# A hybrid decoder trunk on one core: attention norm applied inside TensorE's transposes, and VectorE's program written out for both layers

## The chip, the cores and the metric

The kernel runs on one core of a Trainium2 chip. The metric is the device time of one execution in microseconds (us). Lower is better.

## The reference, cut to what matters

Two layers, one after the other, over 256 tokens with 1024 features, all in fp32. Each layer normalises x, makes one wide projection that feeds three kinds of attention, merges them into x, adds a mixture of experts, and adds a gated embedding:

```python
def rmsnorm(x, g):
    xf = x.astype(jnp.float32)
    y = xf * lax.rsqrt(jnp.mean(xf * xf, axis=-1, keepdims=True) + NORM_EPS)
    return (y * g.astype(jnp.float32)).astype(x.dtype)

def hybrid_layer(x, ...):
    h = rmsnorm(x, attn_norm)
    (a_q, ..., gate_logits) = jnp.split(h @ w_in, IN_OFFSETS, axis=-1)
    ...
    x = x + merged @ w_o
    x = x + hierarchical_moe(rmsnorm(x, ffn_norm), ...)
    x = x + jax.nn.sigmoid(rmsnorm(x, ple_norm) @ w_ple_gate) * (p_i @ w_ple)
```

The mixture has 32 experts in 4 groups. Each token takes the best group and the best two experts in it, so 512 token-expert pairs are spread over 32 experts by comparing router logits.

## The kernel before

The 256 tokens are two tiles of 128 (t = 0, 1), with tokens on the partitions in `x` and `h`. Matmuls need features on the partitions, so each normalised x is transposed into `hT` (8 blocks of 128 features, 256 tokens). The program is written for five engines by hand, and each engine has its own instruction stream; they meet only through semaphores. What the text calls the layer loop is a hardware loop (`Fori`) over the two layers in each of the five streams. A value that a semaphore must reach depends on the layer; inside the hardware loop it is worked out with register instructions.

There are three norms in a layer, and `n` numbers them: 0 attention, 1 experts (ffn), 2 embedding gate (ple). For each tile ScalarE squares x with a running sum and takes the root (`rms_of_x`; all of ScalarE's operations are recorded at line 1210), and sends `rms_ready`. What follows differs:

- Norm 0: VectorE takes the reciprocal (L1500) and writes the normalised tile to `h` (`normed`, L1502, 128x1024), in the block order of the transposes. TensorE transposes the 8 blocks of `h` (`transpose_tile`, L668, with `h_block`).
- Norms 1 and 2: TensorE transposes x itself (`x_block`, every eighth feature), and the reciprocal root is applied later, to the router's logits or to the gate. For norm 1 VectorE still writes `h` with `normed`, since the gather of rows for the experts reads it (L1104).

A tile is transposed in two halves of four blocks, each into one bank of `ps`; VectorE takes each half out with the norm's gain (`take_hT`, L1510). With the four takes of norm 0 done, TensorE starts the wide projection (`channel_group`, L695, then L674 for token-major products).

The layer then goes through the three attention branches, the merge and the output projection (L674). Between the two products of the output projection's second tile TensorE transposes x's tile 0 for the router, and tile 1 when x is updated (L1822 on VectorE). The router's products follow, VectorE picks the experts in a chain of small operations (L1830 to L1885), TensorE gathers (L1104), VectorE takes the gathered rows (L1915), and the expert rounds begin (L1120 for gate and up, L1163 for down). A round handles four experts with up to 32 tokens each. 8 rounds cover the 32 experts; an expert with more tokens than 32 adds rounds, up to 4 more. SyncE issues all weight transfers (L552 for the fixed weights through the three-slot `ring`, L564 for expert weights); a transfer waits until TensorE has used the buffer that it overwrites. The first round's `w_up_e` goes into the buffers of `w_gate_e`, so it waits for the first expert matmuls.

After the rounds comes the embedding gate: VectorE adds the experts' sums to x (L2006), TensorE transposes tile 0, multiplies, transposes tile 1 behind the first products (L1199 is the embedding's product), and VectorE updates x four times (L1517, L2020). Then the next layer starts.

The scratch memory `work` is laid out by hand; `conv_e` ends at 5 * 1024 of its first part, and the next 256 columns are free at a layer's start.

Of the kernel before, what the change touches and what calls it, by code (L numbers as in the profile page):

```python
# [29 lines left out]
ALU = mybir.AluOpType  # L30
# [3 lines left out]
P = 128  # L34
D = 1024
SEQ = 256
T = SEQ // P
# [128 lines left out]
def _build(nc, a, ctx):  # L166
    L_N = a["x_layers"]
# [4 lines left out]
    def signal(name, per=1):  # L172
        return Signal(ctx.enter_context(nc.semaphore(name)), per)
# [15 lines left out]
    ps = ctx.enter_context(nc.psum_tensor("ps", [P, 8, 512], F32))  # L189
# [19 lines left out]
    scratch = Arena(work[:, 0:3 * SLOT])  # L209
# [13 lines left out]
    ident = table("ident")  # L223
# [45 lines left out]
    y_of = [scratch.take(T, 512, at=at) for at in (0, 7 * 1024, 0)]  # L269

    sq_of = [scratch.take(T, 512, at=at) for at in (1024, 2 * 1024)]
    merged = scratch.take(T, D, at=9 * 1024)
    kswap = scratch.take(T, P, at=11 * 1024)
    kTa = scratch.take(SEQ, at=11 * 1024 + 256)
# [73 lines left out]
    rms = sm(T)  # L348
    rstd = sm(T)
# [41 lines left out]
    s_trigd = signal("trig_done")  # L391
    s_zero = signal("zeros_ready")
    s_ss = signal("rms_ready", 3 * T)
    s_h = signal("h_normed")
    s_rs = signal("ple_rstd_ready")
    s_hTp = signal("h_transposed", 3 * 4)
    s_hT = signal("hT_ready", 3 * 4)
# [112 lines left out]
    block = ctx.enter_context(nc.Block())  # L510
# [138 lines left out]
    def _(pe):  # L649
        mm = nc.tensor.matmul  # L650
        tr = nc.tensor.transpose
# [5 lines left out]
        with pe.Fori(0, L_N) as L:  # L657
# [3 lines left out]
            def x_block(t, k):  # L661
                return x[:, t, k:D:KT]

            def transpose_tile(n, block, t):

                for q in range(2):
                    for k in range(4):
                        last = tr(ps[:, 4 + 2 * t + q, k * P:(k + 1) * P], block(t, 4 * q + k), ident)  # L668
                    last.then_inc(s_hTp.sem, 1)

            def token_major(j, t, bank, c0, n, at=0):
# [7 lines left out]
                pe.wait_ge(s_slot[j % 3].sem, slot_loaded(L, j))  # L679

            for t in range(T):
                pe.wait_ge(s_h.sem, L * T + t + 1)
                transpose_tile(0, h_block, t)
            pe.wait_ge(s_hT.sem, s_hT.at(L, 4))

            def channel_group(g):
# [32 lines left out]
            for t in range(T):  # L719
                last = token_major(J_CG, t, 4 + t, 8, 512)  # L720
# [8 lines left out]
            for t in range(T):  # L729
                last = token_major(J_BVT, t, t, 0, 256)  # L730
# [3 lines left out]
            for t in range(T):  # L734
                last = token_major(J_BR, t, 4 + t, 0, 512)
# [4 lines left out]
            for t in range(T):  # L740
                for i, m in enumerate((causal, after, table("chunk0"), table("chunk1"))):
                    last = mm(ps[:, 6, 64 + 16 * t + 4 * i:68 + 16 * t + 4 * i], m, gdec[:, t, :], start=True, stop=True)
# [5 lines left out]
            for t in range(T):  # L748
                for hh in range(H):
                    last = mm(ps[:, 2 + t, hh * P:(hh + 1) * P], gB[:, t, hh, :], causal, start=True, stop=True)  # L750
# [85 lines left out]
            for l in range(LEVELS):  # L836
# [3 lines left out]
                elif l == 4:  # L840

                    pe.wait_ge(s_pj_act.sem, s_pj_act.at(L, 4))
                    for t in range(T):
                        last = mm(ps[:, 0, t * 256:(t + 1) * 256], blrT[:, t * P:(t + 1) * P], wa2[:, :],
                                  start=True, stop=True)
# [224 lines left out]
            for t in range(T):  # L1070
                pe.wait_ge(s_mT.sem, s_mT.at(L, 2 * t + 2))
                for f in range(2):
                    token_major(J_WO0 + f, t, 2 * f + t, 0, 512).then_inc((s_wo, s_static_used)[t].sem, 1)
                    if t == 1 and f == 0:

                        pe.wait_ge(s_x.sem, s_x.at(L, 1))
                        transpose_tile(1, x_block, 0)
            need(J_ROUTER)
            pe.wait_ge(s_hT.sem, s_hT.at(L, 6))
            token_major(J_ROUTER, 0, 4, 0, 36)  # L1080
            pe.wait_ge(s_x.sem, s_x.at(L, 2))
            transpose_tile(1, x_block, 1)
            pe.wait_ge(s_hT.sem, s_hT.at(L, 8))
            token_major(J_ROUTER, 1, 5, 0, 36).then_inc(s_static_used.sem, 1)

# [90 lines left out]


            pe.wait_ge(s_x.sem, s_x.at(L, T + 1))
            transpose_tile(2, x_block, 0)
            w = slot_view(J_PLE)  # L1180
            for t in range(T):
                pe.wait_ge(s_hT.sem, s_hT.at(L, 10 + 2 * t))
                for f in range(2):
                    i = 2 * t + f
                    b = 2 * (i % 2)
                    need(J_PG0 + f)
                    if i < 2:

                        pe.wait_ge(s_x.sem, s_x.at(L, 2 * T))
                    else:  # L1190
                        pe.wait_ge(s_pg.sem, s_pg.at(L, i + 3))
                    last = token_major(J_PG0 + f, t, b, 0, 512)
                    if t == 1:
                        last.then_inc(s_static_used.sem, 1)
                    if i == 0:
                        need(J_PLE)
                        pe.wait_ge(s_pl.sem, L + 1)
                    for k in range(2):
                        last = mm(ps[:, b + 1, :], pinT[:, k, t * P:(t + 1) * P], w[:, k, f * 512:(f + 1) * 512],  # L1199
                                  start=(k == 0), stop=(k == 1))  # L1200
                    last.then_inc((s_pg_p if i < 3 else s_static_used).sem, 1)
                    if i == 0:

                        transpose_tile(2, x_block, 1)


    @block.scalar
# [235 lines left out]
    def _(dve):  # L1443
        v = nc.vector
# [43 lines left out]
        dve.wait_ge(s_x0.sem, 16)  # L1488
        dve.wait_ge(s_trigd.sem, 1)
        dve.wait_ge(s_tab0.sem, 16)  # L1490
        with dve.Fori(0, L_N) as L:
            def reciprocal_rms(n):

                dve.wait_ge(s_ss.sem, s_ss.at(L, n * T + T))
# [2 lines left out]
            def normed(n, t):  # L1497

                dve.wait_ge(s_ss.sem, s_ss.at(L, n * T + t + 1))
                v.reciprocal(rstd[:, t:t + 1], rms[:, t:t + 1])  # L1500
                dve.drain()
                return ts(h[:, t, :].rearrange("p (k d) -> p k d", k=KT), x[:, t, :].rearrange("p (d k) -> p k d", k=KT),  # L1502
                          rstd[:, t:t + 1], None, ALU.mult)
# [13 lines left out]
                return stt(out=out, in0=half_tanh, scalar=1.0, in1=gated, op0=ALU.add, op1=ALU.mult)  # L1517

            for t in range(T):
                normed(0, t).then_inc(s_h.sem, 1)  # L1520
            dve.wait_ge(s_par.sem, 48 * (L + 1))
            for t in range(T):
                take_hT(0, "attn_norm", t)
# [538 lines left out]
```

## Time and profile before

| | us |
|---|---|
| runs of the kernel before | 1835.51, 1855.69, 2714.79 |
| their median | 1855.69 |
| the profiled execution | 1843.19 |
| its span | 1841.5 |
| TensorE matmuls busy | 1456.5 (79%) |
| VectorE busy | 395.5 (21%) |
| ScalarE busy | 218.4 (12%) |

The span is the time from the first to the last record of the profiled execution; its own time is 1.7 us more. Its mean granted TensorE clock was 0.924 of full speed. Busy shares are means over stages that differ: in about half of the span the transfers of expert weights run without a pause, and in the rest TensorE and VectorE take turns. The rows quoted below give a start and a length in us; a bracket behind a row is the time that the engine sat idle before it, and what ended it. A fp32 matmul may be recorded as more than one MATMUL record.

### The profile page before, as it was taken

How to read it: one execution, taken by the hardware profiler on the slowest of the kernel's cores; microseconds unless marked ns; L12 is line 12 of the kernel's file. 1: busy time of each engine (PE TensorE's matmuls, PEld its weight loads, DVE VectorE, ACT ScalarE, POOL GpSimd, SP SyncE). 2: the span in 40 equal slices, each digit the busy share in tenths (PEclk: the TensorE clock that was granted, in tenths of full speed). 3: DMA queues.
4: the chain of work that ended last, by engine and by line, in shares of the span. 5: the costliest groups of instructions: out<-in, count | busy, mean ns of one | idle time of the engine just before them, and what ended most of it. 6: DMA issues, size and time to landing. Idle time of an engine off the chain costs nothing.

```text
span 1841.5 us, 19673 instructions
## 1 busy us (share of the span) xinstructions
PE 1456.5 (79%) x7340; PEld 720.6 (39%) x7341; DVE 395.5 (21%) x756; ACT 218.4 (12%) x417; POOL 38.0 (2%) x36
## 2 busy tenths in 40 slices
PE   7999999997655665566889999999976656665678
PEld 6657645452211221122476676454422212221223
DVE  3342514143000000000233425141420000000002
ACT  2121312110000000000211223111100000000001
POOL 0012000000000000000000110000000000000000
PEclk9999999998888888888989999999988888888889
DMA  7332033389999999999442320333899999999992
GB/s 249 114 137 92 1 137 137 115 353 365 402 410 409 410 410 410 409 410 407 156 145 92 137 92 6 142 127 137 349 364 410 410 409 410 410 410 409 410 398 87
DMA packets 153499, 501.19 MB, mean 272 GB/s; under 512 B 13763, under 2 KB 16229, under 8 KB 152293
## 3 DMA queue, kind: packets, MB, share of 16 engines
q1 hardware_dynamic: 153140, 498.72, 69.7%
q0 software_dynamic: 304, 1.76, 0.2%
q8 instruction: 34, 0.56, 0.1%
q14 instruction: 21, 0.16, 0.0%
HBM read 499.37 MB, written 1.05 MB: 272 GB/s over the span
## 4 chain that ended last, share of the span: by engine, by line
PE 50%; SPq 28%; DMA 14%; issue 4%; DVE 2%; ACT 1%; DVEq 0%; ACTq 0%
SPq L564 27%; PE ps L674 24%; DMA work<-in_w_gate_e 10%; PE ps L695 5%; PE ps L983 5%; PE ps L1120 3%; DMA ring<-in_w_down_e 2%; DMA work<-in_w_up_e 2%; SPq L508 1%; PE ps L816 1%; PE ps L1163 1%; PE ps L828 1%; ACT work L1210 1%; PE ps L1110 1%; PE ps L1104 1%
## 5 line engine op out<-in xcount | busy, mean ns | idle before, releaser
L1120 PE MATMUL ps<-work 128*32 128x512 f32 x2048 | 335.6, 793 | 277.9 <-DMA work<-in_w_up_e 159.3
L674 PE MATMUL ps<-ring,hT 128*128 128x512 f32 (+3 forms) x1152 | 452.3, 548 | 5.5 <-DVE hT L1510 5.5
L674 PEld LDWEIGHTS ps<-ring,hT 128*128 128x128 f32 x1152 | 208.4, 192 | 227.5 <-issue 223.4
L1210 ACT ACTIVATE work<-ps 128x512 f32<-128x512 f32 (+2 forms) x222 | 125.8, 589 | 1296.8 <-PE ps L1150 445.5
L1120 PEld LDWEIGHTS ps<-work 128*32 128x32 f32 x2048 | 65.5, 131 | 543.3 <-DMA work<-in_w_up_e 238.9
L1517 DVE SCALAR_TENSOR_TENSOR work<-work,ps 128x512 f32<-128x512 f32 (+1 forms) x52 | 37.9, 729 | 598.7 <-ACT work L1210 598.7
L1163 PE MATMUL ps<-ring,work 128*32 128x512 f32 x768 | 110.4, 719 | 39.9 <-DMA ring<-in_w_down_e 39.9
L695 PE MATMUL ps<-hT,ring 128*128 128x256 f32 x384 | 86.1, 387 | 1.8 <-DVE hT L1510 1.8
L983 PE MATMUL ps<-ring,work 128*128 128x512 f32 x192 | 84.7, 594 | 2.9 <-ACT work L1210 2.9
L695 PEld LDWEIGHTS ps<-hT,ring 128*128 128x128 f32 x384 | 74.3, 195 | 12.8 <-issue 1.3
L2000 DVE SCALAR_TENSOR_TENSOR work<-work,ps 128x512 f32<-128x512 f32 x16 | 11.0, 688 | 294.8 <-PE ps L1120 294.8
L1104 PEld LDWEIGHTS ps<-work,h 128*128 128x128 f32 x576 | 67.0, 192 | 9.9 <-issue 7.7
L1163 PEld LDWEIGHTS ps<-ring,work 128*32 128x32 f32 x768 | 26.6, 124 | 111.1 <-DMA ring<-in_w_down_e 57.9
L1104 PE MATMUL ps<-work,h 128*128 128x128 f32 x576 | 67.4, 275 | 2.1 <-DVE work L1885 2.1
L1110 PE MATMUL ps<-work 128*128 128x512 f32 x144 | 67.1, 609 | 1.0 <-ACT work L1210 1.0
L983 PEld LDWEIGHTS ps<-ring,work 128*128 128x128 f32 x192 | 36.2, 190 | 47.5 <-issue 47.5
L635 POOL TENSOR_TENSOR work<-work,tab 128x512 f32<-128x512 f32 x24 | 32.9, 1391 | 852.4 <-DVE work L1612 780.0
L1110 PEld LDWEIGHTS ps<-work 128*128 128x128 f32 x144 | 26.2, 192 | 52.1 <-issue 50.7
L1915 DVE TENSOR_TENSOR work<-ps,cols 128x512 f32<-128x512 f32 x36 | 23.2, 686 | 107.2 <-PE ps L1104 107.2
L1163 PE MATMUL ps<-work 128*32 128x512 f32 x256 | 30.8, 598 | 13.8 <-ACT work L1210 13.8
L1210 ACT ACT_TABLE_LOAD x27 | 34.6, 1283 | 2.3 <-DMA tab<-in_tables 1.0
L1539 DVE SCALAR_TENSOR_TENSOR work<-ps,cols,work 128x255 f32<-128x255 f32 (+2 forms) x72 | 29.7, 475 | 2.2 <-issue 1.0
(262 smaller groups left out, 878.7 us busy)
## 6 DMA issues: line engine op xcount, KB each, us to landing
work<-in_w_gate_e SPq DMA_DIRECT2D x256, 512.0 KB, 15.0
work<-in_w_up_e SPq DMA_DIRECT2D x256, 512.0 KB, 14.6
ring<-in_w_down_e SPq DMA_DIRECT2D x192, 512.0 KB, 15.4
ring<-in_w_in SPq DMA_DIRECT2D x26, 2048.0 KB, 8.0
work<-in_w_down_e SPq DMA_DIRECT2D x64, 512.0 KB, 15.4
ring<-in_w_o SPq DMA_DIRECT2D x4, 2048.0 KB, 8.2
ring<-in_w_ple_gate SPq DMA_DIRECT2D x4, 2048.0 KB, 9.8
ring<-in_w_in SPq DMA_DIRECT2D x2, 2080.0 KB, 8.7
```

The costliest lines, as they stand in the source:

```text
L564: sp.dma_start(place[:, j], src).then_inc(signal_.sem, 16)
L635: pool.tensor_tensor(lower[:, t], AT[:, t], table(f"level{l}").unsqueeze(1).broadcast_to([P, 4, P]), ALU.mult).then_inc(s_lv.sem, 1)
L674: last = mm(ps[:, bank, at:at + n], hT[:, k, t * P:(t + 1) * P], w[:, k, c0:c0 + n], start=(k == 0), stop=(k == w.shape[1] - 1))
L695: last = mm(ps[:, b, (m % 2) * SEQ:(m % 2 + 1) * SEQ], w[:, k, m * P:(m + 1) * P], hT[:, k, :], start=(k == 0), stop=(k == KT - 1))
L983: last = mm(ps[:, 2 + t, :], yT[:, k, t * P:(t + 1) * P], w[:, k, f * 512:(f + 1) * 512], start=(k == 0), stop=(k == 3))
L1104: last = mm(ps[:, 4 + k // 4, (k % 4) * P:(k % 4 + 1) * P], h_block(t, k), sel[:, t].rearrange("p j s -> p (j s)"), start=(t == 0), stop=( ...
L1110: last = mm(ps[:, 2 * t + f, :], selwT[:, t * P:(t + 1) * P], ye[:, f * 512:(f + 1) * 512], start=False, stop=False, skip_group_check=True)
L1120: last = mm(ps[CAP * j:CAP * (j + 1), bank, :], xgT[:, 2 * c + k, CAP * j:CAP * (j + 1)], in_slot(c)[:, j, k, :], start=(c + k == 0), stop ...
L1163: last = mm(ps[CAP * j:CAP * (j + 1), 4 + f, :], hgT[:, k, CAP * j:CAP * (j + 1)], down_slot(k)[:, j, f * 512:(f + 1) * 512], start=(k == ...
L1210: return nc.scalar.activation(*args, **kw)
L1517: return stt(out=out, in0=half_tanh, scalar=1.0, in1=gated, op0=ALU.add, op1=ALU.mult)
L1539: last = stt(out=conv_y[:, m, d:], in0=src[:, m, 0:SEQ - d], scalar=w, in1=conv_y[:, m, d:], op0=ALU.mult, op1=ALU.add)
```

## The change

There are two changes in one diff.

First, the attention norm. VectorE no longer writes a normalised copy of x. For each tile it takes the reciprocal root and multiplies the identity (128x128) by it, one value for each partition, into `diag_rstd`. TensorE multiplies each block of x, as the stationary operand, with this diagonal as the moving one, which transposes and scales at once. `h_block` is no longer used there. `transpose_tile` now makes an ordinary matmul (`mm`) of all its blocks in place of `tr`: with the diagonal for norm 0, with the identity for norms 1 and 2.

Second, VectorE's layer loop is a Python loop, so that its instructions are written out twice, with constants where the semaphore values were worked out in registers. The loop over the expert rounds inside it stays a hardware loop. The four other engines keep their layer loop.

```diff
--- before.py
+++ after.py
@@ -269,6 +269,7 @@
     y_of = [scratch.take(T, 512, at=at) for at in (0, 7 * 1024, 0)]
 
     sq_of = [scratch.take(T, 512, at=at) for at in (1024, 2 * 1024)]
+    diag_rstd = scratch.take(T, P, at=5 * 1024)
     merged = scratch.take(T, D, at=9 * 1024)
     kswap = scratch.take(T, P, at=11 * 1024)
     kTa = scratch.take(SEQ, at=11 * 1024 + 256)
@@ -391,7 +392,7 @@
     s_trigd = signal("trig_done")
     s_zero = signal("zeros_ready")
     s_ss = signal("rms_ready", 3 * T)
-    s_h = signal("h_normed")
+    s_h = signal("rstd_diagonal_ready", T)
     s_rs = signal("ple_rstd_ready")
     s_hTp = signal("h_transposed", 3 * 4)
     s_hT = signal("hT_ready", 3 * 4)
@@ -661,11 +662,12 @@
             def x_block(t, k):
                 return x[:, t, k:D:KT]
 
-            def transpose_tile(n, block, t):
+            def transpose_tile(t, by):
 
                 for q in range(2):
                     for k in range(4):
-                        last = tr(ps[:, 4 + 2 * t + q, k * P:(k + 1) * P], block(t, 4 * q + k), ident)
+                        last = mm(ps[:, 4 + 2 * t + q, k * P:(k + 1) * P], x_block(t, 4 * q + k), by,
+                                  start=True, stop=True)
                     last.then_inc(s_hTp.sem, 1)
 
             def token_major(j, t, bank, c0, n, at=0):
@@ -679,8 +681,8 @@
                 pe.wait_ge(s_slot[j % 3].sem, slot_loaded(L, j))
 
             for t in range(T):
-                pe.wait_ge(s_h.sem, L * T + t + 1)
-                transpose_tile(0, h_block, t)
+                pe.wait_ge(s_h.sem, s_h.at(L, t + 1))
+                transpose_tile(t, diag_rstd[:, t, :])
             pe.wait_ge(s_hT.sem, s_hT.at(L, 4))
 
             def channel_group(g):
@@ -1074,12 +1076,12 @@
                     if t == 1 and f == 0:
 
                         pe.wait_ge(s_x.sem, s_x.at(L, 1))
-                        transpose_tile(1, x_block, 0)
+                        transpose_tile(0, ident)
             need(J_ROUTER)
             pe.wait_ge(s_hT.sem, s_hT.at(L, 6))
             token_major(J_ROUTER, 0, 4, 0, 36)
             pe.wait_ge(s_x.sem, s_x.at(L, 2))
-            transpose_tile(1, x_block, 1)
+            transpose_tile(1, ident)
             pe.wait_ge(s_hT.sem, s_hT.at(L, 8))
             token_major(J_ROUTER, 1, 5, 0, 36).then_inc(s_static_used.sem, 1)
 
@@ -1176,7 +1178,7 @@
 
 
             pe.wait_ge(s_x.sem, s_x.at(L, T + 1))
-            transpose_tile(2, x_block, 0)
+            transpose_tile(0, ident)
             w = slot_view(J_PLE)
             for t in range(T):
                 pe.wait_ge(s_hT.sem, s_hT.at(L, 10 + 2 * t))
@@ -1201,7 +1203,7 @@
                     last.then_inc((s_pg_p if i < 3 else s_static_used).sem, 1)
                     if i == 0:
 
-                        transpose_tile(2, x_block, 1)
+                        transpose_tile(1, ident)
 
 
     @block.scalar
@@ -1488,7 +1490,7 @@
         dve.wait_ge(s_x0.sem, 16)
         dve.wait_ge(s_trigd.sem, 1)
         dve.wait_ge(s_tab0.sem, 16)
-        with dve.Fori(0, L_N) as L:
+        for L in range(L_N):
             def reciprocal_rms(n):
 
                 dve.wait_ge(s_ss.sem, s_ss.at(L, n * T + T))
@@ -1517,7 +1519,10 @@
                 return stt(out=out, in0=half_tanh, scalar=1.0, in1=gated, op0=ALU.add, op1=ALU.mult)
 
             for t in range(T):
-                normed(0, t).then_inc(s_h.sem, 1)
+                dve.wait_ge(s_ss.sem, s_ss.at(L, t + 1))
+                v.reciprocal(rstd[:, t:t + 1], rms[:, t:t + 1])
+                dve.drain()
+                ts(diag_rstd[:, t, :], ident, rstd[:, t:t + 1], None, ALU.mult).then_inc(s_h.sem, 1)
             dve.wait_ge(s_par.sem, 48 * (L + 1))
             for t in range(T):
                 take_hT(0, "attn_norm", t)
```

On VectorE, at the head of layer 0 before the change (`small` holds the roots, `h` the normalised x, the row behind is the first take of hT):

```order
L1491 UNCONDITIONAL_BRANCH
L1491 ISA
L1500 RECIPROCAL small<-small 128x1
L1502 TENSOR_SCALAR h<-x,small 128x1024
L1499 REGISTER_ALU
L1500 RECIPROCAL small<-small 128x1
L1502 TENSOR_SCALAR h<-x,small 128x1024
```

and after it (`tab` holds the identity, `work` the diagonal):

```order
L1523 RECIPROCAL small<-small 128x1
L1525 TENSOR_SCALAR work<-tab,small 128x128
L1523 RECIPROCAL small<-small 128x1
L1525 TENSOR_SCALAR work<-tab,small 128x128
L1512 TENSOR_TENSOR hT<-ps,cols 128x4x128 x4
```

The loop's entry and the register instruction are gone, and each 128x1024 operation has become a 128x128 one.

On VectorE, at the end of the layer's code before the change, the last update of x is followed by the loop's register instruction and its jump:

```order
L1517 SCALAR_TENSOR_TENSOR work<-work,ps 128x512
L2020 SCALAR_TENSOR_TENSOR x<-work,x 128x512
L1491 REGISTER_ALU
L1491 COMPARE_AND_BRANCH
L162 UNCONDITIONAL_BRANCH
```

and after it, at the end of layer 0, the next layer's first operations stand directly behind (the `work` of L1525 is the diagonal again):

```order
L1519 SCALAR_TENSOR_TENSOR work<-work,ps 128x512
L2025 SCALAR_TENSOR_TENSOR x<-work,x 128x512
L1523 RECIPROCAL small<-small 128x1
L1525 TENSOR_SCALAR work<-tab,small 128x128
L1523 RECIPROCAL small<-small 128x1
L1525 TENSOR_SCALAR work<-tab,small 128x128
```

On TensorE, at the start of a layer before the change (`tab` is the identity):

```order
L668 MATMUL ps<-tab,h 128x128 x8
L682 REGISTER_ALU
L668 MATMUL ps<-tab,h 128x128 x8
```

and after it:

```order
L669 MATMUL ps<-work,x 128x128 x8
L684 REGISTER_ALU
L669 MATMUL ps<-work,x 128x128 x8
```

The places in the order are the same; the operands are now the diagonal and x.

## Rows read from the trace of the kernel before

**Rows 1.** The page: DMA busy tenths in 40 slices, and a group's busy us.

```profile
DMA  7332033389999999999442320333899999999992
...
L1120 PE MATMUL ps<-work 128*32 128x512 f32 x2048 | 335.6, 793 | 277.9 <-DMA work<-in_w_up_e 159.3
```

**Rows 2.** The chain that ended last: start us, us, what.

```profile
15.80 27.89 PE ps L695 x128
...
569.50 15.51 DMA work<-in_w_gate_e
...
630.94 15.51 DMA work<-in_w_gate_e
...
931.43 30.26 PE ps L695 x128
```

**Rows 3.** The timeline: the first expert matmuls and the weights that they release.

```profile
410.78 7.07 PE L1120 MATMUL ps<-work 128*32 128x512 f32 x64 [1.58 <-DVE work L1915]
...
412.76 11.18 SPq L564 DMA_DIRECT2D work<-in_w_up_e  x16
```

**Rows 4.** Stretches: length, PE, PEld, DVE, ACT, POOL busy, then clock, DMA share, GB/s.

```profile
408.00:412.00 4.00, 2.42 (x23) 1.44 (x25) 2.47 (x12) 0.20 (x1) 0.00 (x0) 1.00 0.03 10
...
922.00:923.00 1.00, 0.00 (x0) 0.00 (x0) 0.00 (x0) 0.93 (x3) 0.00 (x0) 0.80 1.04 406
...
936.00:937.00 1.00, 1.00 (x6) 0.84 (x5) 0.00 (x0) 0.00 (x0) 0.00 (x0) 0.87 0.00 0
```

**Rows 5.** The timeline of the start of layer 0.

```profile
9.93 0.16 DVE L1500 RECIPROCAL small<-small 128x1 f32<-128x1 f32 x1 [4.18 <-ACT small L1210]
...
11.01 0.29 ACT L1210 ACTIVATE small<-small,tab 128x1 f32<-128x1 f32 x1
...
11.34 0.17 DVE L1500 RECIPROCAL small<-small 128x1 f32<-128x1 f32 x1
...
11.38 3.55 PE L668 MATMUL ps<-tab,h 128*128 128x128 f32 x16 [11.38 <-DVE h L1502]
...
14.23 1.42 DVE L1510 TENSOR_TENSOR hT<-ps,cols 128x512 f32<-128x512 f32 x2 [0.16 <-PE ps L668]
15.11 0.69 POOL L621 DMA_DIRECT2D tab<-in_tables  x1 [13.96 <-DMA ring<-in_w_in]
```

**Rows 6.** The timeline of the start of layer 1.

```profile
921.56 0.30 ACT L1210 ACTIVATE small<-small,tab 128x1 f32<-128x1 f32 x1
...
922.96 0.29 ACT L1210 ACTIVATE small<-small,tab 128x1 f32<-128x1 f32 x1
...
925.42 0.17 DVE L1500 RECIPROCAL small<-small 128x1 f32<-128x1 f32 x1 [5.00 <-issue]
925.68 1.14 DVE L1502 TENSOR_SCALAR h<-x,small 128x1024 f32<-128x1024 f32 x1
...
926.88 3.67 PE L668 MATMUL ps<-tab,h 128*128 128x128 f32 x16 [8.67 <-DVE h L1502]
```

**Rows 7.** The timeline of TensorE: eight matmuls at full clock, five transposes at half.

```profile
137.27 1.95 PE L816 MATMUL ps<-work 128*128 128x128 f32 x16
...
927.14 1.27 PE L668 MATMUL ps<-tab,h 128*128 128x128 f32 x5
```

**Rows 8.** The timeline: transposes of x for the router and the embedding gate.

```profile
393.17 1.12 PE L668 MATMUL ps<-tab,x 128*128 128x128 f32 x8
...
393.88 1.29 DVE L1510 TENSOR_TENSOR hT<-ps,cols 128x512 f32<-128x512 f32 x2 [1.52 <-PE ps L668]
...
881.22 1.28 DVE L1510 TENSOR_TENSOR hT<-ps,cols 128x512 f32<-128x512 f32 x2
...
891.41 1.05 PE L668 MATMUL ps<-tab,x 128*128 128x128 f32 x8
```

**Rows 9.** Groups of VectorE by form: busy us, mean ns of one, idle before.

```profile
L1695 DVE TENSOR_SCALAR work<-work 128x512 f32<-128x512 f32 x2 | 0.9, 426 | 0.1
L1901 DVE TENSOR_SCALAR work<-tab,work 128x4 f32<-128x4 f32 x2 | 0.5, 230 | 0.2
```

## The prediction

> **What bounds the kernel now.** I read the page first. Its DMA row has two long stretches of nines, slices 9 to 19 and 30 to 39: the expert stage of each layer, held by the transfers of the expert weights [rows 1]. Everything before those stretches is held by TensorE and by hand-offs to VectorE. The chain of waits says the same: in the expert stage it returns to a `w_gate_e` transfer every 630.94 − 569.50 = 61.44 us, ahead of it stand blocks of matmuls [rows 2]. One round moves four experts.
>
> Then the timeline where the expert stage begins. The router's products end, VectorE picks the experts, the gather and the take of its rows follow, the first expert matmuls start at 410.78, and only they free the buffers for `w_up_e`, whose issues start at 412.76 [rows 3]. From 408 to 412 the DMA engines are 3% busy [rows 4]. So the transfers wait for the compute chain, and a microsecond lost anywhere before 410.78 moves the whole 460 us of transfers by a microsecond. That makes the stages ahead of the experts, and the tail behind them, the place where this change can gain or lose; inside the rounds VectorE waits for others.
>
> Last I read the start of each layer [rows 5, 6]. In layer 0 the reciprocal starts at 9.93, the 1024-wide normalisation follows, TensorE transposes from 11.38, and the last takes of hT end at 14.23 + 1.42 = 15.65; the projection starts at 15.80 [rows 2]. In layer 1 the square root that VectorE needs ends at 921.56 + 0.30 = 921.86, yet its reciprocal starts at 925.42, after 5.00 us idle put down to "issue": it waited for nothing the profile shows. The transposes start at 926.88 and the projection at 931.43 [rows 2]. The clock row falls to half during 922 to 923 (0.80, so at about 922.6) and rises again in 936 to 937 (0.87, so at about 936.26) [rows 4]: 1.2 GHz in between, 2.4 GHz outside.
>
> **Part 1: what a transpose costs now.** The diff turns all 48 transposes of x per layer into ordinary matmuls, not only the 16 of the attention norm. In the rows, an fp32 `transpose` leaves one MATMUL record and an fp32 matmul of the same shape two: L816 issues 8 matmuls per level and has 16 records, L668 issues 8 and has 8. The pace per record is (1.95 − 0.27)/15 = 0.11 us for the matmul [rows 7], and (1.12 − 0.27)/7 = 0.12 for the transpose [rows 8]; at 1.2 GHz it is (1.27 − 0.42)/4 = 0.21 [rows 7] (0.27 and 0.42 are the last record's own length). So each tile of 8 adds 8 records: 0.86 us at full clock, 1.7 at half.
>
> The Trainium skill ("TensorE: Matmul & The Clock Gate", "Terms") says that transpose mode is 4 times faster for FP32; the rows here show twice. I price each matmul at the two records of the rows.
>
> Router, per layer: tile 0 is transposed inside the output projection, where TensorE has no pause: +0.86. Tile 1 starts at 393.17 and VectorE takes its first half at 393.88, its second until 395.17 [rows 8]. With 16 records the last starts 15 × 0.107 = 1.6 us after the first, is done 0.3 later, and one take of 0.65 follows: 2.6 us in place of 2.0, +0.6. Sum +1.45, on the path to 410.78.
>
> Embedding gate at the layer's end: tile 0's takes begin at 881.22 because VectorE adds the other tile of x first, so its longer transposes end under that: 0. Tile 1 stands at 891.41 between dense products, no idle time in its row [rows 8]: +0.86. For two layers, parts so far: 2 × (1.45 + 0.86) = +4.6 us.
>
> **Part 2: the diagonal.** The 128x1024 normalisation takes 1.14 us [rows 6]. A 128x128 multiply by a scalar of each partition has no row. Bounds: 0.23 (128x4, also with a scalar tile) and 0.43 (128x512, constant scalar) [rows 9]. I take 0.25, since the width is nearer to the first; it saves 0.9 us ahead of each first transpose. In the other tile of `x` the wait is for ScalarE anyway.
>
> **Part 3: start of layer 0.** First matmul at 11.38 − 0.9 = 10.48. The rows there run at 0.22 us per record (16 records in 3.55) [rows 5], the half pace, whatever the clock row says, and the projection at 15.80 is at full pace, 4.4 us after the first record. If that holds again, full pace comes at 14.9: 20 records before it, 12 after it in 1.3 us, the last one done at 16.4, its take 17.05, projection 17.15: +1.35. Bounds: half pace to the end gives 10.48 + 31 × 0.215 + 0.45 = 17.6, +0.65 +0.14 = 18.4, that is +2.6. Full pace cannot beat the weights: the queue that waits for the same first chunk goes on at 15.11 [rows 5], so at best −0.65.
>
> **Part 4: start of layer 1.** VectorE's outer loop is written out, so nothing jumps back after layer 0. I remove the idle stretch: reciprocal at 921.90, diagonal done at 922.4, TensorE at 922.44 instead of 926.88. The second diagonal needs ScalarE's second root, 922.96 + 0.29 = 923.25 [rows 6], and is ready at 923.8, while the first tile still runs. What is late next is TensorE, with 32 records. Its own loop still jumps back; its last matmul of layer 0 starts before 918, and I assume that it is ready at 922.4.
>
> Clock: in the trace the clock rose 4.83 us after the dense projection began (931.43 to 936.26). With 922.44 as start that is 927.3: 23 records at 0.213 before it, 9 at 0.107 behind it, done at 928.45, take 929.1, projection 929.25. Gain 2.2 us. The projection then runs at full clock: before, its first 4.83 us ran at half, worth 2.4 us, and the chain has it as 30.26 against 27.89 in layer 0 [rows 2]. Gain 4.6 in all. Bounds: half clock to the end of the transposes, and then as long again in the projection as before: 930.3, gain 1.1. No fall of the clock at all: last transpose 925.8, projection 926.9, gain 6.9.
>
> That the jump makes the 5 us is my reading: the first reciprocal of layer 0 has the same wait and no such stretch, and only a jump lies between. The Trainium skill ("Runtime: NRT & Kernel Launch", "Instruction fetch mechanics") says so too: a taken branch to a target outside the pages held forces a fetch first. Transposes from 926.88 for 3.67 us left the clock at half, and the rise came 4.83 us into dense matmuls; so I count the new matmuls as work that raises it. The Trainium skill ("TensorE: Matmul & The Clock Gate", "Part 4: PE-mode transpose") has transpose mode not counting as busy. By it the rise comes in the transposes, as I forecast; without it, it could come later or sooner, which is the first two rivals.
>
> **Part 5: the rest of the unrolling.** Waits lose their register arithmetic. The second reciprocal of layer 0 has such an instruction before it and starts 0.04 us after ScalarE's result (11.30 to 11.34) [rows 5]: it is done while VectorE waits. I take 0, with −3 us as a bound: some thirty waits on the path at 0.1 us, the gap between the dependent pair at 925.42 and 925.68 (925.59 to 925.68) [rows 6].
>
> **Sum.** +1.35 + 4.6 − 4.6 + 0 = +1.35 us on the profiled execution, 1843.19 (span 1841.5 and 1.7 around it): 1844.5. The three runs of before are 1835.51, 1855.69 and 2714.79, median 1855.69; the profiled time lies between the two low ones, and their distance of 20 us is fifteen times my sum. A difference under 2% (37 us) is about what a measurement of this kernel cannot tell from no change.
>
> **Rivals.**
> - *The half clock stays (slower than before).* Place: both layer starts. If the doubled transposes run at 0.21 us to their end, the starts cost +2.6 and −1.1 and the sum is +2.6 − 1.1 + 4.6 = +6.1: 1849.3. It decides once the clock rises later than 32 × 0.21 = 6.8 us after the first record. For it: 926.88 to 936.26 is 9.4 us at half clock. Against it: layer 0, 4.4 us. Chance 0.16.
> - *The clock never falls, and waits get cheaper.* −0.65 or +1.35 at the first start, −6.9 at the second, −3 in Part 5: about −4, 1839. For it: the fall came at 922.6, and TensorE would start at 922.44. Against it: 0.2 us ahead is little, after 4 us of idling. Chance 0.13.
> - *The idle stretch stays (the writing out does not do its work).* If something other than the jump holds VectorE until 925.42, TensorE starts 0.9 us earlier, at 926.0; by Part 4's counting the transposes end at 932.1, the projection starts at 932.9 (+1.5) and is spared 2.4 of half clock: −0.9 in place of −4.6. Sum +5: 1848. Chance 0.08.
> - *Matmuls at four times the transpose.* 0.43 us for each in place of 0.21. Tiles on the path then add 2.57 instead of 0.86, router 5.0, tail 4.3 per layer, starts, counted as in Parts 3 and 4, +4.8 and −1.1: +22, 1865.5. Against it: [rows 7], where 8 matmuls take 1.95 us. Chance 0.02. (This is the Trainium skill's factor of 4 from "Terms".)
> - *An overflow round (slower by over 2%).* The product with the diagonal rounds otherwise than VectorE's multiply; a token near a tie changes its expert, and if an expert passes 32 tokens one more round runs: 61.44 us [rows 2], 1906. Against it: L1120 has 2048 records, 128 for a round [rows 1], so 16 rounds, 8 for each layer, the least there can be, and rounding differences are tiny. Chance 0.01.
> - *The written-out program stalls.* Layer 1 of VectorE is new code, fetched in sequence as layer 0's is; layer 0 shows no stall of this size. If each block stalled 5 us on the path some four times: +20, 1864. Chance 0.02.
>
> **How the numbers follow.** Forecast 0.58, rivals as above. All but the last three lie in 1839 to 1850 for this one execution; the scatter of undisturbed runs, 1835.5 to 1855.7, is wider and sets the range: 1832 to 1860. Faster by over 2% has no case of its own, only scatter: 0.02. Slower: the overflow round and scatter: 0.03. Within: 0.95.
>
> **What would show it.** L669 (the transposes) with 96 × 2 = 192 records, about 0.11 us apart; VectorE's first reciprocal of layer 1 within 0.1 us of ScalarE's root, without the 5 us; TensorE restarting about 4.4 us earlier there; the layer 1 projection near 27.9; the layer 0 projection starting near 17.1; `w_up_e` about 2.8 us later than 412.76. Wrong would be: one record for each transpose (then the sum is about −6), a new idle stretch at TensorE's own jump, or 17 rounds.

## The result, and the profile after

The changed kernel takes 1863.78 us (median of 6 runs, 1860.25 to 1873.95); the kernel before, timed beside it, 1843.62 us. The ratio is 1.0098, 95% interval 1.0067 to 1.0128: slower by 1%, where a change of +1.35 us was forecast, lost in the scatter, and outside the range of 1832 to 1860. One run of the kernel before in the list, 2714.79 us, was disturbed and is not part of the ratio. The profiled execution of the changed kernel takes 1863.26 us, its span 1861.6 us, 20.1 us more than the span before.

The page of the changed kernel, its DMA row (the columns are those of [rows 1]):

```profile
DMA  6332033389999999999343320434899999999991
```

The two long stretches of nines are as long as before; what grew lies around them. The chain that ended last says where (start us, us, what; it answers to [rows 2]):

```profile
10.60 7.91 PE ps L669 x32
19.37 27.89 PE ps L697 x128
...
385.76 3.67 PE ps L669 x16
...
398.01 3.89 PE ps L669 x16
...
888.85 3.69 PE ps L669 x16
...
904.02 3.67 PE ps L669 x16
...
937.72 7.91 PE ps L669 x32
946.49 27.89 PE ps L697 x128
...
1314.55 3.67 PE ps L669 x16
```

L669 is the transpose of a tile. A tile of 16 records takes 3.7 to 3.9 us, where the tile of 8 took about 1 [rows 8] and 1.9 was forecast. The projection of layer 0 starts 3.6 us later than in [rows 2]; in layer 1 it runs at full clock, 27.89 us in place of 30.26.

To see the whole I read the same points in both traces, the start of the first record of a stage's first matmuls on TensorE, and took differences. "Picked" is the first product that counts the chosen experts, "gather" the first gather, "tail" the first transpose after the rounds, "last gate product" the last record of the embedding's product:

| stage, us | layer 0 before | after | layer 1 before | after |
|---|---|---|---|---|
| start, to the first projection record (in layer 1 from the last gate product) | 15.8 | 19.4 | 13.8 | 13.6 |
| projection and solve, to the products of its result | 169.0 | 167.3 | 171.4 | 169.0 |
| branches and merge, to the merged transposes | 174.8 | 174.8 | 174.8 | 174.8 |
| output projection and router, to picked | 43.4 | 50.8 | 43.3 | 48.9 |
| picked to gather | 2.4 | 2.3 | 2.4 | 2.3 |
| expert rounds, gather to tail | 469.7 | 469.3 | 469.8 | 467.0 |
| tail, to the last gate product | 42.5 | 49.0 | 42.5 | 47.2 |

The differences add up to +20.1 us. The change touches the two starts, the two router stages and the two tails: +3.6, −0.2, +7.4, +5.6, +6.5, +4.7. They make +27.6, so the other stages are 7.5 us shorter in all. Of that 2.4 are the projection of layer 1, and 1.7 are the clock: TensorE falls to 1.2 GHz now and then, for some microseconds, at places that differ from one execution to the next, and in 62 to 66 us it did so before the change and not after it (first the kernel before, then the changed one; length, PE, PEld, DVE, ACT, POOL busy, clock, DMA share, GB/s):

```profile
62.00:66.00 4.00, 4.00 (x11) 2.20 (x11) 3.85 (x10) 0.00 (x0) 0.00 (x0) 0.57 0.99 378
```

```profile
62.00:66.00 4.00, 4.00 (x39) 4.00 (x37) 3.00 (x8) 1.02 (x1) 0.00 (x0) 1.00 0.63 195
```

Layer 1's expert rounds are 2.8 us shorter, which is not explained here; over all profiles of this case such a stage takes 466 to 471 us. In the changed kernel's layer 0 the router's short product fell into a stretch at half clock, and so did the tail's first product. These are stretches of its trace, in the same columns:

```profile
403.00:404.00 1.00, 1.00 (x7) 1.00 (x6) 0.93 (x1) 0.00 (x0) 0.00 (x0) 0.50 1.07 426
...
895.00:896.00 1.00, 1.00 (x3) 0.48 (x2) 0.00 (x0) 0.00 (x0) 0.00 (x0) 0.50 0.02 6
```

That is why those two stages grew by 1.8 us more in layer 0 than in layer 1, and why I use the layer 1 differences for the price: 5.6 for the router, 4.7 for the tail.

The slow part shows at TensorE's weight loads. This is the view of one line (minimum, median and maximum of one instruction in ns, first and last start), first the changed kernel:

```profile
L669 PEld LDWEIGHTS ps<-tab,x x128: 312/334/338, 385.2 to 1830.0; 128*128 128x128 f32 x128
...
L669 PEld LDWEIGHTS ps<-work,x x64: 312/336/340, 10.6 to 945.1; 128*128 128x128 f32 x64
```

and the kernel before, the same blocks of x in transpose mode, and the matmuls whose pace I had taken:

```profile
L668 PEld LDWEIGHTS ps<-tab,x x64: 186/193/256, 383.3 to 1810.1; 128*128 128x128 f32 x64
```

```profile
L816 PEld LDWEIGHTS ps<-work x160: 186/192/193, 136.8 to 1100.6; 128*128 128x128 f32 x160
```

Records doubled as forecast (128 for 64, 64 for 32), but each load takes 334 ns, not 192, and the next record starts about (3.83 − 0.27)/15 = 0.24 us after the last one, not 0.11:

```profile
385.60 3.83 PE L669 MATMUL ps<-tab,x 128*128 128x128 f32 x16
```

(0.27 is the last record's own length.) While these loads run TensorE's loader is busy without a pause, at full clock, which [rows 4] have as 1.00 in the clock column:

```profile
387.00:388.00 1.00, 1.00 (x6) 1.00 (x6) 0.43 (x1) 0.00 (x0) 0.00 (x0) 1.00 1.03 414
```

The start of layer 1, in the timeline of the changed kernel, answers to [rows 6]:

```profile
936.80 0.30 ACT L1212 ACTIVATE small<-small,tab 128x1 f32<-128x1 f32 x1
...
937.13 0.16 DVE L1523 RECIPROCAL small<-small 128x1 f32<-128x1 f32 x1 [1.46 <-ACT small L1212]
937.38 0.29 DVE L1525 TENSOR_SCALAR work<-tab,small 128x128 f32<-128x128 f32 x1
...
937.72 7.90 PE L669 MATMUL ps<-work,x 128*128 128x128 f32 x32 [4.27 <-DVE work L1525]
```

The 5 us "issue" are gone: the reciprocal starts 0.03 us after the root ends at 937.10. TensorE idles 4.27 us in place of 8.67, and then needs 7.90 us for what took 3.67. The gain and the loss of this start are almost equal.

### The profile page after: what moved, and what is told of

Its sections match the earlier page's. It is cut to its first block, busy times and chain, and to the rows that moved or that the text cites. A ratio compares the mean times of both kernels' runs of the same rounds, so it can differ in the third digit from the quotient of the medians.

```text
span 1861.6 us, 19770 instructions
## 1 busy us (share of the span) xinstructions
PE 1470.6 (79%) x7436; PEld 749.6 (40%) x7437; DVE 393.3 (21%) x755; ACT 218.6 (12%) x417; POOL 38.0 (2%) x36
## 3 DMA queue, kind: packets, MB, share of 16 engines
HBM read 499.37 MB, written 1.05 MB: 269 GB/s over the span
## 4 chain that ended last, share of the span: by engine, by line
PE 51%; SPq 29%; DMA 13%; issue 4%; DVE 2%; ACT 1%; DVEq 0%; ACTq 0%
SPq L565 27%; PE ps L676 24%; DMA work<-in_w_gate_e 10%; PE ps L697 4%; PE ps L985 4%; PE ps L1122 2%; PE ps L669 2%; DMA work<-in_w_up_e 2%; DMA ring<-in_w_down_e 2%; SPq L509 1%; PE ps L818 1%; PE ps L1165 1%; PE ps L830 1%; PE ps L1106 1%; PE ps L1112 1%
## 5 line engine op out<-in xcount | busy, mean ns | idle before, releaser
L1122 PE MATMUL ps<-work 128*32 128x512 f32 x2048 | 329.1, 777 | 279.9 <-DMA work<-in_w_up_e 158.5
L1165 PE MATMUL ps<-ring,work 128*32 128x512 f32 x768 | 101.3, 660 | 49.1 <-DMA ring<-in_w_down_e 49.1
L1165 PE MATMUL ps<-work 128*32 128x512 f32 x256 | 30.8, 598 | 13.8 <-ACT work L1212 13.8
L669 PEld LDWEIGHTS ps<-tab,x 128*128 128x128 f32 x128 | 31.4, 332 | 2.3 <-issue 1.0
```

The costliest lines, as they stand in the source:

```text
L669: last = mm(ps[:, 4 + 2 * t + q, k * P:(k + 1) * P], x_block(t, 4 * q + k), by, start=True, stop=True)
L1122: last = mm(ps[CAP * j:CAP * (j + 1), bank, :], xgT[:, 2 * c + k, CAP * j:CAP * (j + 1)], in_slot(c)[:, j, k, :], start=(c + k == 0), stop ...
L1165: last = mm(ps[CAP * j:CAP * (j + 1), 4 + f, :], hgT[:, k, CAP * j:CAP * (j + 1)], down_slot(k)[:, j, f * 512:(f + 1) * 512], start=(k == ...
```

## The experiments

Theory S, formed on these rows: an fp32 matmul loads a stationary operand slowly when its elements lie 8 apart, as in `x_block`. Rival F: it is the form, two records and another operand beside x, whatever the step. A third question was whether the written-out program gives what I thought. All medians below stand beside the kernel before, timed on the same chip in the same job.

**e1, blocks of neighbouring features for the attention norm.** w_in's rows and the gain are read in the matching order. The places of the diff that matter:

```diff
+                order = "l (k p) n -> (l p) k n" if name == "w_in" else "l (p k) n -> (l p) k n"
...
+            def near_block(t, k):
+                return x[:, t, k * P:(k + 1) * P]
...
-                transpose_tile(t, diag_rstd[:, t, :])
+                transpose_tile(t, diag_rstd[:, t, :], near_block)
```

> The changed kernel, but the transposes of the attention norm take blocks of 128 neighbouring features (the order of w_in's rows and of the gain follows); the result is the same. Theory S: an fp32 matmul whose stationary operand has a step of 8 elements runs at 0.23 us per record, and a contiguous one at 0.11 (0.21 at half clock). Then the 64 records with the diagonal have weight loads of about 190 ns in place of 336, the projection of layer 0 starts at 16 to 17.5 in place of 19.37, and the time is about 1859 (1863.8 less 2 to 3 us for each layer start). Theory F: the pace comes from the form (two records, the diagonal or x as operands), not from the step: loads stay at 336 ns, 1864. The transposes of norms 1 and 2 keep step 8 and stay at 0.23 under both.

Measured: 1859.93 us against 1846.11, ratio 1.0072 (1.0050 to 1.0094). The records of the line:

```profile
L673 PEld LDWEIGHTS ps<-tab,x x128: 312/334/338, 390.3 to 1828.1; 128*128 128x128 f32 x128
...
L673 PEld LDWEIGHTS ps<-work,x x64: 192/333/333, 10.4 to 943.1; 128*128 128x128 f32 x64
```

The minimum with the diagonal falls to 192; the median does not, because at half clock a load of neighbouring elements takes 333 too. The lengths tell them apart: 32 records in 6.65 us in layer 0 and 5.36 in layer 1, against 7.91 in both. In layer 0 the first 28 of the 32 records start 0.21 us apart and only the last four 0.11. The clock column reads 1.00 there, as it does for the slow transposes of [rows 5]; that this is half clock is read from the pace. In layer 1 it reads 0.50 for the first half of them. The starts are 17.9 and 11.1 us, against 19.4 and 13.6. Theory S holds for the pace; my expectation of about 190 ns for all 64 was too simple, and 17.9 lies above the 16 to 17.5 that I had for layer 0.

**e2, transpose mode back for norms 1 and 2.**

```diff
+                        out = ps[:, 4 + 2 * t + q, k * P:(k + 1) * P]
+                        if by is ident:
+                            last = tr(out, x_block(t, 4 * q + k), ident)
+                        else:
+                            last = mm(out, x_block(t, 4 * q + k), by, start=True, stop=True)
```

> The changed kernel with transpose mode back for norms 1 and 2; the diagonal stays for norm 0. If the matmul form of these 32 transposes is what cost the time, the router stages give back 7.4 and 5.5 us and the tails 6.4 and 3.1 us (differences of the two chains): 1863.8 - 22 = about 1842. If the written-out program of VectorE is to blame for some of it, the time stays above 1850.

Measured: 1848.16 us against 1846.11, ratio 1.001 (0.998 to 1.004). The tails are 42.5 us in both layers, as before; the router stages are 45.2 and 45.0, about 1.7 above before, each with 6.8 us at half clock in it (layer 0 from 403 us on). So the 32 transposes of norms 1 and 2 account for nearly all of the loss. It came out at 1848 and not at 1842; its profile shows the clock in that (178.1 and 178.0 us in the branches, where the kernel before has 174.8), and whether it is all of it is open.

**e3 and f2, VectorE written out and nothing else.**

```diff
-        with dve.Fori(0, L_N) as L:
+        for L in range(L_N):
```

> The kernel before, with VectorE's layer loop written out and nothing else. If the jump back held VectorE for 3.5 us at the start of layer 1, its first reciprocal follows ScalarE's root within 0.1 us, TensorE restarts about 3.5 us earlier, and the time is 1843.6 - 3.5 to - 6 = about 1839. Rival: the written-out program has stalls of its own: 1845 or more.

> The kernel before with VectorE's layer loop written out, timed a second time beside the run with both repairs: about 1842, a ratio of 0.997 to the kernel before; about 3 us under the other. If the first measurement was scatter, the ratio is 1.0.

Measured: 1841.90 us against 1846.11, ratio 0.9974 (0.9953 to 0.9995), and the second time 1842.53 against 1844.66, ratio 0.9983 (0.9960 to 1.0006). The start of layer 1 is 10.0 us in both profiles, against 13.8, and it is the stretch before the reciprocal that went. This is its timeline in e3:

```profile
927.56 0.29 ACT L1210 ACTIVATE small<-small,tab 128x1 f32<-128x1 f32 x1
...
927.89 0.16 DVE L1500 RECIPROCAL small<-small 128x1 f32<-128x1 f32 x1 [1.46 <-ACT small L1210]
...
929.35 3.42 PE L668 MATMUL ps<-tab,h 128*128 128x128 f32 x16 [5.13 <-DVE h L1502]
...
933.64 2.64 PE L695 MATMUL ps<-hT,ring 128*128 128x256 f32 x11 [0.88 <-DVE hT L1510]
```

The 3.8 us are clear in the trace, and the projection behind them runs at full clock (27.89 us in place of 30.26). In the total the two drown: two measurements of 10 runs each give −4 and −2 us, and the second interval includes no change.

What happens in the stretch shows in the view of the DMA queues, in the packets that carry instructions. From 900 to 1000 us the three kernels with VectorE's loop, the kernel before and e4 and e8 below, have three such packets on queue 14 (packets, MB, share):

```profile
q14 instruction: 3, 0.02, 0.1%
```

The changed kernel and every run with the program written out have none on it there, while the four on queue 8 are in all. The first of the three starts at 923.32 in the kernel before and at 939.60 in e8, each 2.1 us ahead of the late reciprocal (925.42 and 941.71). So a transfer of VectorE's own instructions goes with the jump back and goes away with it; that queue 14 is VectorE's is read from this match, and how the 3.6 us divide into the transfer and the rest stays open.

**e4, matmul in place of transpose mode in the kernel before.** It has `h` (neighbouring elements) and `x` (step 8) side by side.

```diff
-                        last = tr(ps[:, 4 + 2 * t + q, k * P:(k + 1) * P], block(t, 4 * q + k), ident)
+                        last = mm(ps[:, 4 + 2 * t + q, k * P:(k + 1) * P], block(t, 4 * q + k), ident,
+                                  start=True, stop=True)
```

> The kernel before, with an ordinary matmul with the identity in place of transpose mode in all 48 transposes of x or h in a layer; the loop and the normalised copy stay. One kernel has both kinds: h is contiguous, x has step 8. Theory S: records from h have weight loads of 190 ns and a pace of 0.11 (0.21 at half clock), those from x 332 ns and 0.23. Theory F: both 332 ns. Time under S: 1843.6 + 22 for norms 1 and 2 (as in the changed kernel) + 2 to 4 for norm 0 = about 1868; under F about 1872.

Measured: 1867.39 us against 1846.11, ratio 1.0118 (1.0080 to 1.0155), as theory S had it. Its router stages take 50.6 us and its tails 47.2. The 32 records of h at the start of layer 0 take 6.34 us, against 7.91 for x in the changed kernel. In both layers TensorE spent part of the router stage at half clock (10.2 us in layer 0), which fits the 50.6 here beside the 48.9 in layer 1 of the changed kernel, where it did not.

**e8, the changed kernel with VectorE's loop kept.**

> The changed kernel with VectorE's layer loop back: diagonal and matmuls stay. If the jump back holds VectorE, its first reciprocal of layer 1 comes about 3.5 us after ScalarE's root and the start of layer 1 (last gate product to first projection) takes 13.6 + 3.5 = 17.1 us; all else as in the changed kernel. If the written-out code was not what removed the stretch, it takes 13.6.

Measured: 1877.0 us in one run, beside 1850.43. The reciprocal of layer 1, in its timeline:

```profile
941.71 0.16 DVE L1523 RECIPROCAL small<-small 128x1 f32<-128x1 f32 x1 [5.08 <-issue]
```

ScalarE's root ended at 937.76 + 0.30 = 938.06, so the 3.65 us are back, and the start of layer 1 takes 17.3 us where 17.1 was expected. Its total is higher than those 3.7 us explain: other stages of its profile are 1 to 3 us longer too (the branches of layer 1 take 178.1 in place of 174.8, its tail 48.9 in place of 47.2), and it is a single run, so I draw only the start from it. Whether the loop costs anything elsewhere is open.

**e5 and e6, other steps.** The blocks are cut with a step of 1, 2, 4 or 8 elements, and the rows of the weight and the gain are laid out to match.

```diff
+            def block_of(step):
+                def block(t, k):
+                    at = k // step * step * P + k % step
+                    return x[:, t, at:at + (P - 1) * step + 1:step]
+                return block
```

> The changed kernel with other steps between the elements of a block of x: 2 for the attention norm's transposes (the rows of w_in and the gain are laid out to match), 8 as before for the router's, 4 for the embedding gate's (w_ple_gate laid out to match). The result is the same. If any step over 1 brings the slow load, all three stay at 0.23 us per record at full clock (loads of 312 ns or more). If the cost grows with the step, step 2 runs at about 0.11 to 0.13 and step 4 between that and 0.23. If only the step of 8 elements (32 bytes) is slow, steps 2 and 4 both run at 0.11 and the tails shrink from 47.2 to about 44.3 us.

> The same with step 4 for the attention norm, 8 for the router, 1 for the embedding gate. Step 1 at full clock in the tail: 0.11 us per record, loads of 190 ns, a tail of 42.5 + 0.9 = 43.4 us in place of 47.2. Step 4: as in the run with steps 2, 8 and 4; the layer start tells it a second time: 32 records in 7.9 us if slow, 5.4 to 6.7 if not.

Measured, one run each: 1859.74 and 1854.93 us, beside 1850.43. The line's records, in e5 step 2 (layer 0's start) and step 4 (layer 0's tail):

```profile
L676 PEld LDWEIGHTS ps<-work,x x32: 195/197/331, 10.5 to 15.5; 128*128 128x128 f32 x32
...
L676 PEld LDWEIGHTS ps<-tab,x x32: 308/329/332, 890.8 to 907.7; 128*128 128x128 f32 x32
```

and in e6 step 4 (layer 0's start) and step 1 (layer 0's tail):

```profile
L676 PEld LDWEIGHTS ps<-work,x x32: 309/329/329, 10.7 to 17.9; 128*128 128x128 f32 x32
...
L676 PEld LDWEIGHTS ps<-tab,x x32: 186/192/192, 889.5 to 902.9; 128*128 128x128 f32 x32
```

| step | load at full clock, ns | a tile of 16 records at full clock, us |
|---|---|---|
| 1 | 192 | 1.95 |
| 2 | 197 | not measured in a tail |
| 4 | 329 | 3.77 |
| 8 | 334 | 3.83 |

None of the three expectations was right as a whole: the cost is neither there from step 2 on nor at 8 alone. Step 2 costs 5 ns more than step 1 and is otherwise free of it, 4 and 8 pay it in full: for fp32 the cost sets in between 8 and 16 bytes from one element to the next. No other type was run, and what in the load takes the time no run here tells. The 32 records of a layer's start take 5.35 us with step 2 and 7.73 with step 4. With step 1 the tail of e6 is 43.4 and 43.5 us: 42.5 + 0.9, the price that my prediction gave to it.

**f1, both repairs.** Neighbouring blocks for the diagonal, transpose mode for norms 1 and 2, VectorE written out.

> Both repairs at once: the diagonal for the attention norm on blocks of neighbouring features, transpose mode for the 32 transposes of norms 1 and 2, VectorE written out. If the slow load and the doubled records are all that the change cost, the stages are those of the runs that had them apart: start of layer 0 about 17.9 us, of layer 1 about 11.1, router 43.4 to 45.2, tail 42.5. Against the kernel before that is +2.1, -2.7 and -2.4 (the projection at full clock), 1846.1 - 3 = about 1843; against the kernel with only VectorE written out (1841.9), slower by 2.3 + 1.1 = about 3. If the diagonal is a gain of its own beside it, it comes below 1840.

Measured: 1841.71 us against 1844.66, ratio 0.9966 (0.9941 to 0.9990). Its starts are 17.8 and 11.2 us, its router stages 43.5 and 43.4, its tails 42.5 in both layers, so each repair does beside the other what it did alone. It is as fast as f2, timed in the same job (1842.53); that its starts take 2.0 and 1.2 us longer than f2's (15.8 and 10.0) is not to be seen in the medians. So beside the written-out program the diagonal is no gain in any run: VectorE is done 0.9 us sooner, and the doubled records take more than that. Against the kernel before its gain is 3 us with an interval just below 1; against the changed kernel, 1863.78 in another job, it is some 22 us.

## Why the prediction was wrong, point by point

- **What bounds the kernel.** Right. The expert rounds kept their length within 3 us and moved as a block; the loss sits in the stages ahead of them and in the tails.
- **Part 1, the price of a transpose: this is the step that failed.** I counted the records rightly (two in place of one, 192 in all) and took 0.11 us per record from L816 [rows 7]. That line's stationary operand has its elements side by side. The new matmuls load blocks with a step of 8, and no matmul of the trace did that; the only rows with that step were in transpose mode, where the load takes 193 ns. I took their speed as a property of the block, when it was a property of the mode together with the block. The trace of before even had a sign of it. Its transposes of blocks with neighbouring elements (L706) load in 141 ns where those of x take 193; in transpose mode the longer load does not slow the records, which start 0.11 us apart in both:

```profile
L706 PEld LDWEIGHTS ps<-tab,work x48: 139/141/143, 43.3 to 996.8; 128*128 128x128 f32 x48
L706 PE MATMUL ps<-tab,work x48: 272/272/273, 43.5 to 996.9; 128*128 128x128 f32 x48
```

  The measured pace is 0.24. For each tile it makes +2.8 us in place of +0.86: router +5.6 in place of +1.45 a layer, tail +4.7 in place of +0.86, of which 1.9 us are tile 0's, which I had at nothing because VectorE's addition hid a tile of 1.9 us but not one of 3.8. I should have given this unknown a bound from both sides; I gave none, and so the range was too narrow above.
- **Part 2, the diagonal.** 0.29 us, forecast 0.25 within 0.23 to 0.43.
- **Part 3, start of layer 0.** Forecast 17.15, at most 18.4; measured 19.37. The same step: 32 records at 0.24 take 7.9 us at either clock. Without the slow loads the start was 17.8 to 17.9 (step 1, e1 and f1), still 0.7 above the forecast but within its bound: 28 records ran at half pace there and not the 20 that I counted. With step 2 (e5) full pace came earlier and the start was 16.8.
- **Part 4, start of layer 1.** The mechanism was right: the stretch belongs to the jump back, it goes with the written-out program (e3) and returns with the loop (e8), a transfer of instructions goes and returns with it, and TensorE's own jump was not in the way. The projection ran at full clock, −2.4 us as forecast. The start itself was to gain 2.2 us and gained 0.2, again by the slow loads; e3, without them, gained 3.8.
- **Part 5, the waits.** 0 was right as far as e3 shows: its untouched stages are those of the kernel before within 0.3 us, or lie 1.6 to 1.8 or 3.3 us above where TensorE spent longer at half clock; its rounds are 0.3 and 1.3 shorter.
- **The sum again with the measured pace.** Two layers of 5.6 + 4.7, +3.6, −0.2 and −2.4 make +21.6; measured +20.1 in the span and +20.2 between the medians of the same job (1863.78 less 1843.62). That they agree so closely is partly luck: layer 0's 1.8 and 1.8 more, and the 1.7 and 2.8 us by which other stages got shorter, are not in this sum.
- **The rivals.** "Matmuls at four times the transpose" had 0.43 us for a matmul and 1865.5 us, and both came close: a matmul takes 2 × 0.24 us, the transpose 0.11, and the time was 1863.78. Its reason did not. The same matmul with step 1 takes 2 × 0.11 (e6), twice the transpose, as Part 1 read it; the other factor of two is the step of the load. The Trainium skill's factor of 4 for FP32 ("TensorE: Matmul & The Clock Gate", "Terms") is near what the load with step 8 gives here (0.48 against 0.11 us, 4.4 times), and not what steps 1 and 2 give. Half clock was no reason for the loss: it came for 3.4 us in the start of layer 1 and changed nothing there, since the slow load has the same pace at either clock. No further round ran: 16 again. Of the signs that I named, the reciprocal 0.03 us behind the root, TensorE's restart 4.4 us earlier and the projection of 27.9 us came; the pace of 0.11, the projection of layer 0 at 17.1 and `w_up_e` 2.8 us later did not (it came at 422.01, 9.25 us later).

## What to carry to other kernels

Before a transpose-mode operation is replaced by a matmul, look at the step of its stationary operand as well as at its number of records: fp32 blocks cut with a step of 4 or 8 elements cost here 3.8 us for 8 matmuls, side by side 1.95, in transpose mode 1.05 with a step of 8 and no more side by side. A helper that several callers share should be changed only for the one that may gain: the 16 transposes with the diagonal saved VectorE 0.9 us ahead of TensorE, the 32 others had nothing to win. Even the 16 were no gain here: with neighbouring elements (f1) the two starts are 2.0 and 1.2 us longer than with transposes of `h` (f2). And where a price is read from a row of another line, the layout of the operands is part of the row; if no row has that layout, the term needs a bound for it.

## What the runs showed that I had not expected

- **The step of the load.** 192 and 197 ns with steps 1 and 2, 329 and 334 with 4 and 8, all at full clock. At half clock a load with step 1 takes 333 as well, so the slow load hides the clock: its pace is the same at both.
- **Transpose mode and the clock.** My fourth part let only ordinary matmuls raise the clock. In e3 TensorE ran nothing but transposes from 929.35 to 932.8, and the clock, at half since about 929.0, rose in 932 to 933, before any ordinary matmul of the layer:

```profile
930.00:931.00 1.00, 1.00 (x7) 1.00 (x6) 1.00 (x2) 0.86 (x3) 0.00 (x0) 0.50 1.04 383
...
932.00:933.00 1.00, 0.77 (x5) 0.53 (x3) 0.84 (x3) 0.00 (x0) 0.00 (x0) 0.81 1.06 391
```

  In f2, the same program, the clock likewise rose at 934.1, while the transposes that began at 931.38 still ran. So a layer start with transposes alone can reach full clock in time for the projection. It need not: in the kernel before the transposes from 926.88 to 930.55 left it at half until 936.26. The statement of the Trainium skill ("TensorE: Matmul & The Clock Gate", "Part 4: PE-mode transpose") that transpose mode does not bring the full clock is not borne out by these two runs, with fp32 blocks; the measurement decides.
- **Where the scatter of the total comes from.** In most profiles some stage ahead of the experts spends a few microseconds at half clock: in e3 the state scan of layer 0, from about 202 to 209 (0.59 and 0.72 in its stretches), which made that stage 178.1 us in place of 174.8. The projection stage takes 167.3, 169.0, 170.6 or 172.4 us from one profile to another. e3 and f2 are the same program, and they differ in this way: 45.2 and 43.6 us in layer 0's router stage, 174.8 and 178.1 in layer 1's branches. Differences of 2 to 4 us between kernels are therefore read from the stages, not from the medians.

```profile
201.00:206.00 5.00, 4.45 (x16) 3.28 (x17) 1.19 (x2) 2.72 (x6) 0.00 (x0) 0.59 0.00 0
206.00:211.00 5.00, 4.43 (x26) 3.67 (x24) 1.67 (x3) 0.88 (x8) 0.00 (x0) 0.72 0.01 3
```
